# Gated DeltaNet input: beta and decay as the first unit of the gate's stretch, key and query norms inside the gate's units

## The reference

```
proj = x @ w_in                                   # q, k, v: 3072 columns, z: 1024, b: 8, a: 8
qkv  = silu(causal_dwconv([conv_buf, qkv], conv_w))
q, k = l2_normalize(q) * dk ** -0.5, l2_normalize(k)      # per head, over its 128 entries
beta = sigmoid(b)
g    = -exp(a_log) * softplus(a + dt_bias)        # log decay, then a cumulative sum in each chunk
...
o    = rms_norm(o, o_norm) * silu(z)              # z is the gate
```

## Time and profile before

| | before |
|---|---|
| time, median of 3 runs | 2835.37 us (2835.32 to 2835.97) |
| time of the profiled execution | 2833.51 us |
| its span, first to last instruction | 2831.7 us |
| granted TensorE clock, mean | 0.962 |
| busy: PE, weight load (PEld), DVE, ACT, POOL | 93%, 90%, 40%, 31%, 37% |
| chain that ended last, by engine | PE 81%, issue 9%, DVE 6%, POOL 3%, ACT 2% |
| transfers | 202.82 MB, 72 GB/s |

### The profile page before, as it was taken

One profiled execution on the slowest core, in us unless ns is written; L12 is line 12 of the kernel. 1 busy time (PEld: TensorE's weight loads), 2 busy tenths in 40 slices (PEclk: granted clock), 3 DMA queues, 4 the chain that ended last, 5 costly groups with the idle time before them and its releaser, 6 DMA issues.

```text
span 2831.7 us, 61615 instructions
## 1 busy us (share of the span) xinstructions
PE 2625.3 (93%) x26993; PEld 2540.6 (90%) x26993; DVE 1125.1 (40%) x1390; ACT 870.4 (31%) x1207; POOL 1035.3 (37%) x479
## 2 busy tenths in 40 slices
PE   7999999997899999999999999899488887999997
PEld 7999998996888899999899998898378857999997
DVE  3333117845544433321433321721844464433312
ACT  4222223332333422222322222334533323322221
POOL 3444442433434344444244444133043214244432
PEclk9999999998998999999999999899699998999998
DMA  4222221221013222322222222122000012122321
GB/s 144 86 89 98 92 75 61 89 65 38 2 61 112 68 82 88 97 93 78 62 88 89 94 91 84 45 76 82 1 4 4 4 72 89 53 89 89 98 89 45
DMA packets 53585, 202.82 MB, mean 72 GB/s; under 512 B 6320, under 2 KB 6448, under 8 KB 53424
## 3 DMA queue, kind: packets, MB, share of 16 engines
q1 hardware_dynamic: 53424, 200.38, 21.6%
HBM read 190.68 MB, written 9.67 MB: 71 GB/s over the span
## 4 chain that ended last, share of the span: by engine, by line
PE 81%; issue 9%; DVE 6%; POOL 3%; ACT 2%; DMA 0%; SPq 0%; POOLq 0%; DVEq 0%; ACTq 0%
PE ps L334 21%; PE ps L332 21%; PE ps L333 21%; PE ps L350 2%; PE ps L351 2%; POOL wlo L302 2%; PE ps L352 2%; PE ps L2229 1%; PE ps L2237 1%; DVE sFM L2407 1%; PE ps L650 1%; PE ps L388 1%; PE ps L2180 1%; PE ps L2185 1%; PE ps L2288 1%
## 5 line engine op out<-in xcount | busy, mean ns | idle before, releaser
L302 POOL TENSOR_TENSOR wlo<-raw,whi 128x1024 fp32r<-128x1024 f32 (+1 forms) x265 | 719.1, 2714 | 1189.8 <-ACT whi L277 1189.8
L332 PE MATMUL ps<-xh,whi 128*128 128x272 f32 x3632 | 1050.2, 289 | 11.9 <-POOL wlo L302 10.9
L334 PE MATMUL ps<-xh,wlo 128*128 128x272 f32 x3632 | 1054.3, 290 | 0.0
L333 PE MATMUL ps<-xl,whi 128*128 128x272 f32 x3632 | 1046.6, 288 | 0.0
L332 PEld LDWEIGHTS ps<-xh,whi 128*128 128x128 f32 x3632 | 686.1, 189 | 15.1 <-POOL wlo L302 7.9
L333 PEld LDWEIGHTS ps<-xl,whi 128*128 128x128 f32 x3632 | 687.1, 189 | 0.0
L334 PEld LDWEIGHTS ps<-xh,wlo 128*128 128x128 f32 x3632 | 684.9, 189 | 0.0
L277 ACT ACTIVATE whi<-raw 128x1024 fp32r<-128x1024 f32 (+1 forms) x265 | 301.8, 1139 | 1137.6 <-PE ps L334 1117.5
L334 PE MATMUL ps<-mh,wlo 128*128 128x272 f32 x1408 | 406.1, 288 | 0.0
L333 PE MATMUL ps<-ml,whi 128*128 128x272 f32 x1408 | 405.4, 288 | 0.0
L332 PE MATMUL ps<-mh,whi 128*128 128x272 f32 x1408 | 405.0, 288 | 0.0
(11 more groups left out here) (457 smaller groups left out, 3202.5 us busy)
## 6 DMA issues: line engine op xcount, KB each, us to landing
raw<-w SPq DMA_DIRECT2D x249, 512.0 KB, 3.5
raw<-w SPq DMA_DIRECT2D x64, 704.0 KB, 4.1
mS<-state_gdn SPq DMA_DIRECT2D x8, 512.0 KB, 5.0
gdn_s_s<-mS SPq DMA_DIRECT2D x8, 512.0 KB, 2.8
h<-xT SPq DMA_DIRECT2D x4, 544.0 KB, 7.8
yT<-h SPq DMA_DIRECT2D x4, 544.0 KB, 2.7
go_r<-w SPq DMA_DIRECT2D x4, 512.0 KB, 5.4
S<-state_rwkv SPq DMA_DIRECT2D x8, 256.0 KB, 4.1
```

What stands on the lines that cost most here:

```text
L302: pool.tensor_tensor(wlo[two][:, 0:kt * P], raw[slot][:, 0:kt * P], whi[two][:, 0:kt * P].bitcast(F32), ALU.subtract).then_inc(w_lo, 1)
L332: pe.matmul(o, wh, hi[:, r, :], start=(start and k == 0), stop=False)
L333: pe.matmul(o, wh, lo[:, r, :], start=False, stop=False)
L334: mm = pe.matmul(o, wl, hi[:, r, :], start=False, stop=(stop and k == kt - 1))
```

## The change

The unit `ba` moves ahead of the gate units, which become a product of their own, `gdn_z`, behind it. The sums of the norms move into gate units 1 and 2, one after every second step (6 products); the spreads move into gate units 4 to 7, one after every fourth step (12 products). The transposes of beta and decay stand ahead of gate unit 2, the second products ahead of gate unit 4. The gate units alternate between two pairs of banks (`z_pair`), the spreads between the other two. ACT squares all tiles beside units 1 and 2, runs the root, beta and decay behind that, and the silus of the gate at the end (`gates`), in two batches. DVE scales the gate units between the steps of the decay (`z_dve`) and clears the states ahead of the first multiplication. Number, shape and type of the matrix products stay as they are.

```diff
 PRODUCTS = [
...
-    ("gdn_in", 4 * HG, NM), ("ba", 1, NM), ("gdn_out", NM, NM),
+    ("gdn_in", NQKV, NM), ("ba", 1, NM), ("gdn_z", HG, NM), ("gdn_out", NM, NM),
...
 def unit_mm(..., between=None):
...
-                mm.then_inc(acc, 1)
+                    if k == kt - 1:
+                        mm.then_inc(acc, 1)
+                    if between is not None:
+                        between(half * kt + k)
...
 def gdn_in_act(act):
...
             body(0, True)
-            with act.Fori(1, NQKV // 4) as i:
+            with act.Fori(1, NQKV // 4 - 1) as i:
                 body(i, False)
+            for j, (name, unit) in enumerate((("gdn_in", 2), ("gdn_in", 3), ("ba", 0), ("gdn_z", 0))):
+                split_hi(act, name, NQKV - 4 if name == "gdn_in" else 0, unit)
+                silu_out(NQKV - 5 + j, 1 - j % 2)
             silu_out(NQKV - 1, 1)
-            for i in range(2):
...
+        def z_act(act):
+            def squares(tiles):
+                for t in tiles:
+                    act.wait_ge(S["qkv_ready"], t + 1)
+                    if t > 1:
+                        act.wait_ge(S["l2_mm"], t - 1)
+                    act.activation(tb[t % 2][:, :, :], qkv[:, 2 * t:2 * t + 2, :], ACT.Square).then_inc(S["l2_sq"], 1)
+
+            def z_hi(m):
+                split_hi(act, "gdn_z", m - m % 4, m % 4)
...
+            squares(range(2))
+            z_hi(1)
+            z_hi(2)
+            squares(range(2, HG))
+            z_hi(3)
+            squares(range(HG, 2 * HG))
+            z_hi(4)
+            l2_act(act)
+            ba_act2(act)
+            z_hi(5)
+            ba_act3(act)
+            z_hi(6)
+            gates(range(4))
+            z_hi(7)
+            gates(range(4, HG))
...
+        def z_pair(m):
+            return pair((m + 1) % 2)
+
+        def z_dve(dve, m):
+            dve.wait_ge(acc, 2 * (BASE["gdn_z"] + m + 1))
+            dve.tensor_tensor(zg[:, 2 * m:2 * m + 2, :], z_pair(m), rs[:, :, :], ALU.mult).then_inc(S["z_scaled"], 1)
...
 def gdn_in_pe(pe):
...
+            pe.wait_ge(S["ext_ready"], NQKV - 1)
+            unit_mm(pe, "ba", 0, 0, pair(0), xh, xl)
             for m in range(HG):
...
+                if m == 0:
+                    pe.wait_ge(S["ext_ready"], NQKV)
+                elif m == 1:
+                    pe.wait_ge(S["gdn_dve"], 2)
+                    pe.wait_ge(S["cv"], 5 * NQKV)
                 else:
+                    pe.wait_ge(S["z_scaled"], m - 1)
+                if m == 2:
+                    ba_pe_transpose(pe)
+                if m == 4:
+                    ba_pe_second(pe)
+
+                def between(step):
+                    if m in (1, 2) and step % 2 == 1:
+                        l2_sum(pe, HG * (m - 1) + step // 2)
+                    if m >= 4 and step % 4 == 3:
+                        l2_spread(pe, 4 * (m - 4) + step // 4)
+                unit_mm(pe, "gdn_z", m - m % 4, m % 4, z_pair(m), xh, xl, between=between)
+            pe.wait_ge(S["z_scaled"], HG)
...
 def l2_ba_dve(dve):
...
-            dve.tensor_tensor(tb[3][0:16, :, :], pair(2)[0:16], rs[0:16, :, :], ALU.mult).then_inc(d, 1)
-            dve.wait_ge(S["l2_rt"], 1)
-            dve.reciprocal(ROOTS, ROOTS).then_inc(S["l2_rs"], 1)
+            dve.tensor_tensor(tb[3][0:16, :, :], pair(0)[0:16], rs[0:16, :, :], ALU.mult).then_inc(d, 1)
+            z_dve(dve, 0)
+            z_dve(dve, 1)
...
-            l2_dve(dve, range(4))
-
+            z_dve(dve, 2)
+            dve.wait_ge(S["l2_rt"], 1)
+            dve.reciprocal(ROOTS, ROOTS).then_inc(S["l2_rs"], 1)
             dve.wait_ge(S["gdn_act"], 5)
...
-            l2_dve(dve, range(4, 12))
+            z_dve(dve, 3)
             dve.wait_ge(S["gdn_pe"], 1)
...
             dve.memset(Sst[:, :, :], 0.0).then_inc(S["s_up"], 1)
             dve.memset(SG[:, :, :], 0.0).then_inc(S["o_cp"], 1)
-            l2_dve(dve, range(12, 2 * HG))
+            for m in range(4, HG):
+                l2_dve(dve, range(4 * m - 16, 4 * m - 12))
+                z_dve(dve, m)
             dve.wait_ge(S["gdn_act"], 6)
...
```

More of the change, by code:

```diff
@@ L316, in pool_units, with unit_mm @@
                 body(4 * i, False)
-        def unit_mm(pe, name, u, j, out, hi, lo, k0=0, start=True, stop=True, ready=None):
+        def unit_mm(pe, name, u, j, out, hi, lo, k0=0, start=True, stop=True, ready=None, between=None):
             base, kt = BASE[name], KT[name]
@@ L803, in gdn_in_act, with gates @@
             body(0, True)
-            with act.Fori(1, NQKV // 4) as i:
+            with act.Fori(1, NQKV // 4 - 1) as i:
                 body(i, False)
+            for j, (name, unit) in enumerate((("gdn_in", 2), ("gdn_in", 3), ("ba", 0), ("gdn_z", 0))):
+                split_hi(act, name, NQKV - 4 if name == "gdn_in" else 0, unit)
+                silu_out(NQKV - 5 + j, 1 - j % 2)
             silu_out(NQKV - 1, 1)
-            for i in range(2):
[L808 to L819, removed]
+        def z_act(act):
[7 more added lines that the diff above has]
+                split_hi(act, "gdn_z", m - m % 4, m % 4)
+            def gates(ms):
+                for m in ms:
                     act.wait_ge(S["z_scaled"], m + 1)
                     act.activation(zg[:, 2 * m:2 * m + 2, :], zg[:, 2 * m:2 * m + 2, :], ACT.Silu).then_inc(S["z_ready"], 1)
+            squares(range(2))
[13 more added lines that the diff above has]
+            gates(range(4, HG))
         def gdn_in_dve(dve):
@@ L864, in gdn_in_dve @@
                 body(i, False)
-            for m in range(HG):
-                dve.wait_ge(acc, 2 * (BASE["gdn_in"] + NQKV + m + 1))
-                dve.tensor_tensor(zg[:, 2 * m:2 * m + 2, :], pair(m % 3), rs[:, :, :], ALU.mult).then_inc(S["z_scaled"], 1)
+        def z_pair(m):
[3 more added lines that the diff above has]
+            dve.tensor_tensor(zg[:, 2 * m:2 * m + 2, :], z_pair(m), rs[:, :, :], ALU.mult).then_inc(S["z_scaled"], 1)
         def gdn_in_pe(pe):
@@ L877, in gdn_in_pe, with l2_sum @@
                     unit_mm(pe, "gdn_in", i * 4, j, pair(j % 2), xh, xl)
+            pe.wait_ge(S["ext_ready"], NQKV - 1)
+            unit_mm(pe, "ba", 0, 0, pair(0), xh, xl)
             for m in range(HG):
[L880 to L883, removed]
-                else:
[L885 to L896, removed]
+                if m == 0:
[3 more added lines that the diff above has]
+                    pe.wait_ge(S["cv"], 5 * NQKV)
+                else:
+                    pe.wait_ge(S["z_scaled"], m - 1)
[10 more added lines that the diff above has]
+            pe.wait_ge(S["z_scaled"], HG)
+        def l2_sum(pe, t):
+            pe.wait_ge(S["l2_sq"], t + 1)
+            sum_rows(pe, 6, one_col[:, 31 - t:63 - t], tb[t % 2], t == 0, t == 15).then_inc(S["l2_mm"], 1)
         def l2_act(act):
@@ L902, in l2_act, with l2_spread @@
             act.activation(ROOTS, row_sums(6), ACT.Sqrt, bias=eps[:, 0:1]).then_inc(S["l2_rt"], 1)
[L904 to L911, removed]
+        def l2_spread(pe, t):
+            if t == 0:
+                pe.wait_ge(S["l2_rs"], 3)
+            if t > 1:
+                pe.wait_ge(S["l2_done"], t - 1)
+            spread_row(pe, pair(2 + t % 2), t).then_inc(S["l2_bc"], 1)
         def l2_dve(dve, tiles):
@@ L916, in l2_dve @@
                 q = qkv[:, 2 * t:2 * t + 2, :]
-                dve.scalar_tensor_tensor(q, q, P ** -0.5 if t < HG else 1.0, pair(t % 2), ALU.mult, ALU.mult).then_inc(S["l2_done"], 1)
+                dve.scalar_tensor_tensor(q, q, P ** -0.5 if t < HG else 1.0, pair(2 + t % 2), ALU.mult, ALU.mult).then_inc(S["l2_done"], 1)
         PIECES = [(P, slice(0, NCH), list(range(NCH))), (NS, slice(NCH, NCH + 1), [NCH])]
-        def ba_pe_first(pe):
-            unit_mm(pe, "ba", 0, 0, pair(2), xh, xl)
         def ba_pe_transpose(pe):
@@ L952, in ba_act2, with ba_act3 @@
             act.activation(gs["gc"][:, 0, :], vec[:, V_ALOG:V_ALOG + HG], ACT.Exp).then_inc(S["gdn_act"], 1)
+        def ba_act3(act):
             act.wait_ge(S["gdn_dve"], 9)
@@ L1679, in gdn_pe @@
             gdn_in_pe(pe)
[L1680 to L1685, removed]
             prompt_pe(pe)
@@ L1695, in gdn_act @@
             gdn_in_act(act)
-            l2_act(act)
-            ba_act2(act)
+            z_act(act)
             act.wait_ge(S["cn_out"], 16)
@@ L1717, in gdn_pool @@
             split_lo(pool, "ba", 0, 0)
+            pool_units(pool, "gdn_z")
             prompt_pool(pool)
@@ L1731, in gdn_sp @@
             load_units(sp, "ba")
+            load_units(sp, "gdn_z")
             sp.wait_ge(S["conv_done"], NQKV)
@@ L2899, in lay_out @@
     ba = np.concatenate([gin[:, 4096:], np.zeros((D, P - 2 * HG), np.float32)], 1)
-    o["w8"] = np.concatenate([ffn_in[0], units(gin[:, :4096]), units(ba), units(f(inp["gdn_w_out"])[0]), ffn_in[1],
+    o["w8"] = np.concatenate([ffn_in[0], units(gin[:, :3072]), units(ba), units(gin[:, 3072:4096]), units(f(inp["gdn_w_out"])[0]), ffn_in[1],
```

2 lines of the change are left out of this document (1 added, 1 removed).

## The result

| | before | after |
|---|---|---|
| time, median of 12 runs each | 2834.27 us (2828.56 to 2838.25) | 2839.11 us (2835.05 to 2841.57) |
| after / before | | 1.0018, 95% interval 1.0010 to 1.0026 |
| profiled execution, its span | 2833.51, 2831.7 us | 2841.22, 2839.4 us |
| last q/k/v unit's end to the first prompt product | 85.81 us | 91.45 us |

The kernel is 0.18% slower, about 5 us. The size was forecast at 6.0 us, and the time lies in the range, 0.7 us above its lower end. It is just under the 0.2% at which I had drawn the line between slower and no difference; with twelve runs each the interval excludes no difference, so that line was drawn too wide.

A forecast was written before the change was run, and what follows sets the result against it. PE was taken to bound the kernel. A prompt start 3.0 us later, 1.3 for a table load and 1.7 for the clock summed to 6.0 us slower, 2841.4 us on the median, range 2838.4 to 2844.7.

The forecast's parts named there:

- The gate's first weights: Gate unit 1: two squares ahead of ACT's weight copy make PE start at 601.4, after waiting 2.1 us.
- The sums: Gate units 1 and 2: each norm sum standing alone costs 0.58 us; 16 make 9.2, 2.9 more than in pairs.
- The wait ahead of the second products: Ahead of gate unit 4: PE waits 3.9 us for ACT's decay chain, which starts only behind the last sum.
- The end: Last spread to prompt: DVE scales the last gate unit in between, 0.67 us more; prompt starts at 676.1.
- The table load: Prompt's first exponential: the gates' silu forces a table reload between Abs and Exp, 1.3 us on the path.
- The clock: Gate unit 4: empty wait and small products lower the clock to 0.50, costing 1.7 us, bounds 0 and 3.3.
- Costed at nothing: Weight loads, POOL subtractions, state loads and gate silus stay covered; a late weight would hold PE up to 3.7 us.
- a second slow stretch: Rival: another low-clock stretch behind gate unit 1's wait, or a longer one in unit 4; 7.7 us slower, chance 0.14.
- The clock stays up: Rival, gate unit 4: granted clock 1.00 behind the second products; 4.3 us slower, within 0.2%, chance 0.24.
- the drain: Rival, ACT's table switches: each also costs a drain of 1.38 us, adding 8.3 us; 2849.7 us, chance 0.01.
- the table is there in time: Rival, prompt's first exponential: its table load is off the path; 4.7 us slower, within 0.2%, chance 0.13.
- the packing works as drawn: Rival: no waits ahead of units 1 and 4, no slow stretch; 1.5 us less, chance 0.04; 5.7 us faster, 0.04.

The follow-up runs named there:

- The first experiment: Changed kernel with ACT copying gate unit 1's weights ahead of the first two squares; stretch from mark to prompt 91.67 us, against 91.45.
- early decay: Changed kernel with sigmoid, exponentials and logarithm of beta and decay among unit 2's squares, DVE's decay steps earlier; stretch to the prompt 84.75 us, against 91.45.
- touched table: Changed kernel with a one-column exponential on ACT behind the gate's last silu, loading the table early; stretch to the prompt 91.48 us.
- pairs: Changed kernel with two tiles' sums together after every fourth step in gate units 1 and 2; stretch to the prompt 88.47 us, against 91.45.
- wait only: Changed kernel keeping the wait ahead of gate unit 4, with the second products taken into unit 4 behind its first three steps; stretch 92.47 us.
- all four edits: Changed kernel with unit 1's weights before the squares, decay functions among squares, exponential's table touched ahead, sums paired; ratio to before 0.9980, stretch 81.52 us.
- further arrangement: Changed kernel with the four single edits, plus earlier transposes, other places for decay functions, earlier last gate scaling; ratio to before 0.9971, stretch 79.55 us.
- early clearing: Kernel before with DVE clearing the two states ahead of the fifth multiplication instead of the thirteenth; ratio to before 0.9995, stretch 84.46 us.

## Why the prediction was right, step by step

- **The gate's first weights.** Forecast: PE starts unit 1 at 601.4, 14.1 us behind the mark. Measured 14.0 (588.87 to 602.89). The first experiment shows that the two squares make 1.05 of the 2.04 us. The other 0.99 is the hole that the kernel before had too and filled in part with the first sums.
- **The sums.** Forecast 0.58 us for each, from the norm's interleaved row. Measured 0.57 (1.32 less six products). In pairs they cost 0.79 for two. (Sixteen at 0.58 make 9.3, not the 9.2 of the sum.) For the transposes and the ninth square together 0.7 us were forecast, and unit 2 began its sums 0.5 late.
- **The wait ahead of the second products.** Forecast 3.9 us, measured 3.68. The early decay shows that the chain on ACT behind the last sum makes it.
- **The spreads.** Forecast 2.425 us a period from the output norm, measured 2.43.
- **The end.** Forecast 2.7 us from the last spread's start to the prompt, measured 2.70; moving the last scaling gave 0.63 of it back.
- **The table load.** Forecast 1.3, measured 1.24 from the two distances; the touch ahead takes it away.
- **The clock.** This is the term that was mis-sized: "between them I take a stretch like today's, 1.7". It was 6.6 us at 0.50, and the second products (2.67 us instead of 2.10) and unit 4 (12.2 instead of 9.7) lost 3.1 us, near the upper bound of 3.3. So the profiled stretch is 6.9 us worse, the table load included (5.64 and 1.24), where 6.0 were forecast. The reason given, that the wait and the small products together lower it, was half right: the wait alone does.
- **Costed at nothing.** That held: from 642.6 to 679.0 no late weight holds up PE, the state loads begin at 662.09 and are first read at 847.9, and the last silu of the gate ends at 680.80, ahead of the prompt's Abs at 683.77.

The median moved by 4.8 us, less than the 6.9 of the profiled stretch. Runs of one kernel lie about 10 us apart (12 among 29 runs of the kernel before), and the profiled run after is above its median (2841.22 against 2839.11), so one profile can't give the mean of such terms; the interval of the ratio, 2.8 to 7.4 us, holds both. That the total came so near to 6.0 is in part luck: the clock's term was 1.4 us too small, the others together 0.5 too large, and the median moved by 2 us less than the profile. The chances put most weight on more than 5.7 us; the measured 0.18% lies just under that.

Of the rivals, "a second slow stretch", in its second form (a longer one in unit 4), is what the trace shows: 3.1 us, where that rival had 3.4 and the forecast 1.7. Its total of 7.7 us was too high all the same. "The clock stays up" fell, as did the drain; "the table is there in time" fell until the touch was added; "the packing works as drawn" came true only in the versions that take the waits out.

## What to carry to other kernels

Work that is packed into the holes of the engine that bounds needs its inputs early: before packing, write down when the chain on the other engines that feeds each inserted piece can start, because an insertion that waits in program order stalls everything behind it. Price an inserted group of small products by a row where it already stands between products of the other kind, not by its block, and insert groups as large as the buffers allow. When an activation of another table moves behind the last use of a table, look who needs that table next, and touch it while the engine is idle.

## What the runs showed of the hardware that was not expected

A wait of 3.4 to 3.7 us on PE ahead of gate unit 4 was followed by a clock of 0.50 in all five profiles that have it (kernel after, weights ahead of the squares, touched table, pairs, wait only). In the three without it (early decay, all four edits, further arrangement) the same block of small products left the clock at 1.00. In two of the five (weights ahead of the squares, wait only) the clock fell before the wait ended, so before any small product, and stayed at 0.50 for about 10 us; in the other three it fell 1.0 to 1.2 us behind the wait's end and stayed for about 6.7 us.

Where the clock falls is not set by the program alone. Up to the mark PE runs the same code in all eleven profiles. Among the first q/k/v units a low stretch begins between 469 and 473 us in seven of them and near 479 us in four (kernel after, early decay, touched table, pairs). In these four it costs 1.5 us: from ACT's weight copy at about 472 us to the second copy behind it, which follows PE, it takes 14.4 instead of 12.9 us. So where two profiles differ in the clock, one of each doesn't show that the edit is the cause. This holds for the block of small products between spreads (0.50 behind it in the kernel before and with early clearing, 1.00 when it is spread out) and for the 2.32 us wait (1.00 behind it in the kernel before, 0.50 when the products ahead of it are spread out). What decides there is left open.
